# Adding an expert's rows to a copy of h in DRAM by an indirect DMA instead of scattering them on TensorE

## The reference, cut to what matters

```python
def moe_swiglu(x, w_router, w_in, w_out):      # x: 256 tokens x 1024
    logits = (xt @ w_router)
    top_v, top_i = lax.top_k(logits, 2)        # 2 of 8 experts for each token
    gates = one_hot(top_i) * softmax(top_v)    # summed over the two: 256 x 8
    for e in range(8):                         # w_in[e]: 1024 x 7168, w_out[e]: 3584 x 1024
        y = y + gates[:, e:e + 1] * swiglu(xt, w_in[e], w_out[e])
...
h = h + moe_swiglu(rms_norm(h, m_norm_g[j]), m_w_router[j], m_w_in[j], m_w_out[j])
```

## Time and profile before

| | |
|---|---|
| median of 3 runs | 1932.05 us (1930.89 to 1932.68) |
| the profiled execution | 1930.93 us, of which the trace's span is 1928.9 us |
| TensorE busy | 1882.8 us, 98% of the span |
| DVE busy | 1438.2 us, 75% |
| ACT busy | 1217.9 us, 63% |
| POOL busy | 32.4 us, 2% |
| chain that ended last | PE 93%, DVE 3%, ACT 3% |
| DMA | 508.12 MB, mean 263 GB/s over the span |

### The profile page before, as it was taken

One profiled execution on the slowest core, in us unless ns is written; L12 is line 12 of the kernel. 1 busy time (PEld: TensorE's weight loads), 2 busy tenths in 40 slices (PEclk: granted clock), 3 DMA queues, 4 the chain that ended last, 5 costly groups with the idle time before them and its releaser, 6 DMA issues.

```text
span 1928.9 us, 25964 instructions
## 1 busy us (share of the span) xinstructions
PE 1882.8 (98%) x8896; PEld 1569.7 (81%) x8896; DVE 1438.2 (75%) x1660; ACT 1217.9 (63%) x1360; POOL 32.4 (2%) x49
## 2 busy tenths in 40 slices
PE   8999999999998999999999999999999999999998
PEld 7998888888786888888888888888888878777887
DVE  5565476557666889888898888988989885577643
ACT  5544365447754777677777777777777765556542
POOL 2000000000000000000000000000000000000000
PEclk9999999999998999999999999999999999999999
DMA  8655555554247999999999999999999953345551
GB/s 266 181 189 202 191 185 186 177 176 155 104 143 274 363 383 353 376 365 363 385 349 376 363 364 384 351 376 366 365 380 350 373 204 121 110 135 160 175 176 43
DMA packets 234949, 508.12 MB, mean 263 GB/s; under 512 B 14332, under 2 KB 54352, under 8 KB 234880
## 3 DMA queue, kind: packets, MB, share of 16 engines
q1 hardware_dynamic: 232304, 499.70, 73.0%
q0 software_dynamic: 2272, 6.47, 1.1%
q10 hardware_dynamic: 304, 1.05, 0.2%
HBM read 505.07 MB, written 2.10 MB: 263 GB/s over the span
## 4 chain that ended last, share of the span: by engine, by line
PE 93%; DVE 3%; ACT 3%; issue 1%; DMA 0%; DVEq 0%; SPq 0%; ACTq 0%
PE G L1338 23%; PE G L1340 23%; PE G L1339 22%; PE SM L1338 5%; PE SM L1340 5%; PE SM L1339 5%; PE T L1298 3%; PE T L1724 1%; PE SM L1332 1%; ACT dense_high L453 1%; PE SM L1506 1%; DVE e_low L663 0%; PE G L1845 0%; DVE dense_low L464 0%; PE SM L1704 0%
## 5 line engine op out<-in xcount | busy, mean ns | idle before, releaser
L663 DVE TENSOR_TENSOR e_low<-e_arrived,e_high 128x2048 fp32r<-128x2048 f32 x338 | 756.1, 2286 | 81.1 <-ACT e_high L658 80.6
L658 ACT CAST e_high<-e_arrived 128x2048 fp32r<-128x2048 f32 x338 | 623.9, 1914 | 0.9 <-PE G L1340 0.8
L1338 PE MATMUL G<-e_high,work_r 128*128 128x512 f32 x896 | 355.8, 397 | 4.7 <-DVE routing L2473 4.7
L1340 PE MATMUL G<-e_high,work_r 128*128 128x512 f32 x896 | 350.1, 391 | 0.0
L1339 PE MATMUL G<-e_low,work_r 128*128 128x512 f32 x896 | 349.5, 390 | 0.0
L1338 PE MATMUL G<-dense_high,xT_hi_all 128*128 128x512 f32 (+1 forms) x760 | 295.9, 389 | 4.9 <-DVE dense_low L464 3.7
L1340 PE MATMUL G<-dense_high,xT_lo_all 128*128 128x512 f32 (+1 forms) x760 | 285.1, 375 | 0.0
L1339 PE MATMUL G<-dense_low,xT_hi_all 128*128 128x512 f32 (+1 forms) x760 | 284.1, 374 | 0.0
L464 DVE TENSOR_TENSOR dense_low<-dense_raw,dense_high 128x2048 fp32r<-128x2048 f32 (+1 forms) x74 | 150.5, 2059 | 99.7 <-ACT dense_high L446 97.7
L1338 PEld LDWEIGHTS G<-e_high,work_r 128*128 128x128 f32 x896 | 168.7, 188 | 40.0 <-issue 4.9
L1340 PEld LDWEIGHTS G<-e_high,work_r 128*128 128x128 f32 x896 | 168.6, 188 | 36.3
(11 more groups left out here) (336 smaller groups left out, 2076.3 us busy)
## 6 DMA issues: line engine op xcount, KB each, us to landing
e_arrived<-in_m_w_in_dram SPq DMA_DIRECT2D x448, 512.0 KB, 5.0
e_arrived<-in_m_w_out_dram SPq DMA_DIRECT2D x224, 512.0 KB, 5.0
dense_raw<-in_a_w_in_dram SPq DMA_DIRECT2D x32, 768.0 KB, 4.9
dense_raw<-in_f_w_in_dram SPq DMA_DIRECT2D x44, 512.0 KB, 4.6
dense_raw<-in_w_up_dram SPq DMA_DIRECT2D x16, 1024.0 KB, 5.2
dense_raw<-in_w_down_dram SPq DMA_DIRECT2D x16, 1024.0 KB, 4.8
dense_raw<-in_a_w_out_dram SPq DMA_DIRECT2D x12, 1024.0 KB, 4.9
dense_raw<-in_f_w_out_dram SPq DMA_DIRECT2D x11, 1024.0 KB, 4.9
```

Of the source, the lines that this page charges most:

```text
L658: nc.scalar.copy(e_hi_unit(n), e_raw(n, e_arrived)).then_inc(e_hi, 1)
L663: nc.vector.tensor_tensor(e_raw(n, e_low), e_raw(n, e_arrived), e_hi_unit(n).bitcast(F32), ALU.subtract).then_inc(e_lo, 1)
L1338: nc.tensor.matmul(bank, x_hi, w_hi, start=start, stop=False)
L1340: return nc.tensor.matmul(bank, x_lo, w_hi, start=False, stop=stop)
```

## The change

A second DRAM tensor `sums` (256 rows and 128 spare ones) takes a copy of `h` ahead of the loop. At the end of a pass ACT multiplies the expert's rows by a column of gates, one per slot (`row_gate`), into `y_rows`, and in the next pass POOL adds these rows to `sums` by an indirect DMA that accumulates (`compute_op=ALU.add`), with the row numbers in `row_to`; slots that hold no token go to a spare row of their own. Row numbers and gates come from four small fp32 matmuls behind unit 1 (`row_slots`) into bank T0 and three DVE operations of one column behind the making of units 6 and 7. Since `e_turn(it, 0)` writes T0 again, it now waits for these (`slots_ready`). `y_lo`, both scatters of a pass and DVE's four additions to `h` go out of the loop; only the last expert's rows are still split, scattered and added on chip, on top of the `h` that POOL brings back from `sums`. The turn of `pick` ("route") stays in the loop.

```diff
+        sums = nc.dram_tensor("sums", (S + P, D), F32, kind="Internal").ap()
...
+            for c in range(NT):
+                pool.dma_start(sums[c * P:(c + 1) * P, :], h[:, c, :]).then_inc(rows_saved, 16)
-            pool.wait_ge(rows_saved, 16 * NT)
+            pool.wait_ge(rows_saved, 32 * NT)
...
             with pool.Fori(0, rounds * E) as it:
+                pool.wait_ge(y_taken, it * 2 + 2)
+                pool.wait_ge(slots_ready, it + 1)
+                pool.sem_inc(sums_asked, 1)
+                pool.indirect_dma_start(sums, bass.IndirectOffsetOnAxis(row_to[:, :], 0), y_rows, None, compute_op=ALU.add
+                                        ).then_inc(sums_added, 16)
                 pool.wait_ge(index_ready, it + 1)
...
+            pool.wait_ge(sums_added, rounds * (16 * E))
+            for c in range(NT):
+                pool.dma_start(h[:, c, :], sums[c * P:(c + 1) * P, :]).then_inc(sums_landed, 16)
...
-                act.wait_ge(scatter_full, it * 4 + 4)
+                act.wait_ge(sums_added, it * 16 + 16)
                 for b in range(2):
                     act.wait_ge(y_full, it * 2 + b + 1)
-                    nc.scalar.copy(y_hi[:, b * BANK:(b + 1) * BANK], SM[b][:, :]).then_inc(y_hi_ready, 1)
+                    nc.scalar.mul(y_rows[:, b * BANK:(b + 1) * BANK], SM[b][:, :], row_gate[:, 0:1]).then_inc(y_taken, 1)
+            act.wait_ge(y_taken, rounds * (2 * E) + 2)
+            for b in range(2):
+                nc.scalar.copy(y_hi[:, b * BANK:(b + 1) * BANK], SM[b][:, :]).then_inc(y_hi_ready, 1)
...
+            def row_slots(it):
+                pe.wait_ge(gates_ready, 1)
+                pe.wait_ge(pick_ready, it + 1)
+                pe.wait_ge(e_turned_lo, it * DOWNS)
+                for c in range(NT):
+                    nc.tensor.matmul(T[0][:, 0:2], pick[:, c, :], token_one[:, c, :], start=(c == 0), stop=(c == NT - 1))
+                for c in range(NT):
+                    ins = nc.tensor.matmul(T[0][:, 2:3], pick[:, c, :], gate[:, c, bass.ds(it + 1, 1)], start=(c == 0), stop=(c == NT - 1))
+                ins.then_inc(slots_full, 1)
...
             def e_turn(it, what):
                 g = TURN_OF[what]
+                if what == 0:
+                    pe.wait_ge(slots_ready, it + 2)
...
                         if s == 0 and part == 1:
-                            pe.wait_ge(y_lo_ready, it * 2 + 2)
-                            scatter(0, scatter_full, SM)
-                        if s == 0 and part == 3:
-                            pe.wait_ge(scatter_added, it * 4 + 2)
-                            scatter(1, scatter_full, SM)
+                            row_slots(it)
...
-            V.memset(y_hi.bitcast(F32), 0.0)
-            V.memset(y_lo.bitcast(F32), 0.0).then_inc(y_lo_ready, 1)
-            V.memset(routeT.bitcast(F32), 0.0).then_inc(y_lo_ready, 1)
+            V.memset(y_rows, 0.0).then_inc(y_taken, 2)
+            dve.wait_ge(token_ready, 2)
+            V.tensor_scalar(minus_spare[:, :], spare_row[:, :], -1.0, None, ALU.mult)
+            V.tensor_copy(row_to[:, :], spare_row[:, :]).then_inc(slots_ready, 1)
...
-                    if kind == "up" and s == 0:
-                        c = part // 2
-                        for b in range(2):
-                            dve.wait_ge(scatter_full, it * 4 + 2 * c + b + 1)
-                            dst = h[:, c, b * BANK:(b + 1) * BANK]
-                            V.scalar_tensor_tensor(out=dst, in0=SM[b][:, :], scalar=gate[:, c, bass.ds(it, 1)], in1=dst,
-                                                   op0=ALU.mult, op1=ALU.add).then_inc(scatter_added, 1)
+                    if (kind, s, part) == ("up", 1, 0):
+                        dve.wait_ge(slots_full, it + 1)
+                        dve.wait_ge(sums_added, it * 16 + 16)
+                        V.tensor_copy(row_gate[:, :], T[0][:, 2:3])
+                        steps_loop(V.scalar_tensor_tensor(out=sum_row[:, :], in0=T[0][:, 1:2], scalar=minus_spare[:, 0:1], in1=spare_row[:, :],
+                                                          op0=ALU.mult, op1=ALU.add), it)
+                        V.tensor_tensor(row_to[:, :], T[0][:, 0:1], sum_row[:, :], ALU.add).then_inc(slots_ready, 1)
...
-                for b in range(2):
-                    dve.wait_ge(y_hi_ready, it * 2 + b + 1)
-                    at = slice(b * BANK, (b + 1) * BANK)
-                    V.tensor_tensor(y_lo[:, at], SM[b][:, :], y_hi[:, at].bitcast(F32), ALU.subtract).then_inc(y_lo_ready, 1)
+            for b in range(2):
+                dve.wait_ge(y_hi_ready, b + 1)
+                at = slice(b * BANK, (b + 1) * BANK)
+                V.tensor_tensor(y_lo[:, at], SM[b][:, :], y_hi[:, at].bitcast(F32), ALU.subtract).then_inc(y_lo_ready, 1)
+            dve.wait_ge(sums_landed, 16 * NT)
```

More of the change, by code:

```diff
@@ L255, in build @@
         pos_i = sb("pos_i", [P, NT], I32)
-        token = sb("token", [P, NT])
+        token_one = sb("token_one", [P, NT, 2])
+        token = token_one[:, :, 0]
         token_of = sb("token_of", [P, 1], U32)
+        spare_row, minus_spare, row_gate, sum_row = (routing[:, n:n + 1] for n in range(152, 156))
+        row_to = sb("row_to", [P, 1], U32)
+        sums = nc.dram_tensor("sums", (S + P, D), F32, kind="Internal").ap()
         saved_rows = nc.dram_tensor("saved_rows", (S, D), F32, kind="Internal").ap()
@@ L545, in build @@
         token_ready = sem("token_ready")
+        gates_ready = sem("gates_ready")
+        slots_full = sem("slots_full")
+        slots_ready = sem("slots_ready")
+        sums_asked = sem("sums_asked")
+        sums_added = sem("sums_added")
+        sums_landed = sem("sums_landed")
+        sums_wanted = sem("sums_wanted")
         rows_saved = sem("rows_saved")
@@ L556, in build @@
         y_hi = work_r[:, 0:D]
+        y_rows = work_all[:, 0:D]
+        y_taken = sem("y_taken")
+        row_step = sem("row_step")
         routeT = work_r[:, 1024:1280]
@@ L837, in _ @@
                           allow_slow_non_contiguous=True).then_inc(small_landed, 16)
-            nc.gpsimd.iota(token[:, :], pattern=[[P, NT]], base=0, channel_multiplier=1,
+            steps.then(nc.gpsimd.memset(token_one[:, :, :], 1.0))
+            nc.gpsimd.iota(token, pattern=[[P, NT]], base=0, channel_multiplier=1,
+                           allow_small_or_imprecise_dtypes=True).then_inc(token_ready, 1)
+            nc.gpsimd.iota(spare_row[:, :], pattern=[[0, 1]], base=S, channel_multiplier=1,
                            allow_small_or_imprecise_dtypes=True).then_inc(token_ready, 1)
@@ L854, in _ @@
                                         ).then_inc(rows_landed, 16)
+            pool.wait_ge(sums_added, rounds * (16 * E))
+            pool.sem_inc(sums_wanted, 1)
+            for c in range(NT):
+                pool.dma_start(h[:, c, :], sums[c * P:(c + 1) * P, :]).then_inc(sums_landed, 16)
         @block.scalar
@@ L1725, in e_turn @@
                 ins.then_inc(e_turned, 1)
-            pe.wait_ge(token_ready, 1)
+            pe.wait_ge(token_ready, 2)
             pe.wait_ge(pick_ready, 1)
@@ L1764, in _ @@
                         if s == 0 and part == 0:
-                            pe.wait_ge(scatter_added, it * 4 + 4)
+                            pe.wait_ge(y_taken, it * 2 + 2)
                         if s == DOWNS - 2 and part == 1:
@@ L1783, in _ @@
             for b in range(2):
-                pe.wait_ge(y_lo_ready, rounds * (2 * E) + 2)
+                pe.wait_ge(y_lo_ready, b + 1)
                 pe.wait_ge(gathered[b], rounds * (2 * E) + 2)
@@ L2469, in _ @@
                                                   op0=ALU.mult, op1=ALU.add))
-            steps.then(V.tensor_copy(gate[:, :, E + 1:2 * E + 1], gate[:, :, 1:E + 1]))
+            V.tensor_copy(gate[:, :, E + 1:2 * E + 1], gate[:, :, 1:E + 1]).then_inc(gates_ready, 1)
             dve.wait_ge(rounds_ready, 1)
@@ L2473, in _, with steps_loop @@
             V.memset(tmp8, 0.0).then_inc(up_read, 2)
+            def steps_loop(ins, it):
+                ins.then_inc(row_step, 1)
+                dve.wait_ge(row_step, it + 1)
             with dve.Fori(0, rounds * E) as it:
```

## The result

The changed kernel takes 1965.21 us (median of 4 runs, 1959.69 to 1966.79); beside it the kernel before took 1932.31 (4 runs). The ratio is 1.0167, with a 95% interval of 1.0149 to 1.0185: the change costs 33 us (1.7%). The forecast was 1966, with a range of 1953 to 1980.

What follows compares the result with a forecast made beforehand. TensorE, busy all 121.20 us of a pass, sets the pace, but ACT and DVE feed it at some units. 24.0 wait + 9.6 clock - 0.3 head + 0.5 tail = 33.8 on 1930.9: 1964.7, median 1966, range 1953 to 1980.

Steps and rivals of the forecast that it cites:

- The wait: Ahead of the hidden block's turn, TensorE waits for DVE's slots_ready: 3.0 us a pass, 24.0 in eight.
- The clock: Behind the new idle of 3.8 us TensorE drops to half clock: 1.6 us in 6 of 8 passes, 9.6.
- a choice between two rows: Trace rows on clock loss after TensorE idles: lost after 4.69 us, kept after 2.57 us.
- The removed matmuls: Scatters behind units 1 and 3: 64 matmuls, 14.5 us, their effect already inside the 24.0 us of waiting.
- the full count: Rival: TensorE is full, so removed and added matmuls count in full, -6.5 us, 1925.5; chance 0.04.
- The four small ones: New row-number and gate matmuls behind unit 1: 1.0 us, covered by the wait for unit 2's low part.
- The add: POOL's accumulating DMA into sums: 16.4 us, bounds 8.2 to 24.6, hidden under a cover of 19.6 us.
- the rival built on it: The add lands late at DVE's wait, 5.0 us more per pass and more clock loss, 2012 us; chance 0.10.
- The traffic: The add's bytes beside the weights: 0.5 MB moved up to three times per pass of 42 MB, costing nothing.
- The head: Ahead of the loop, DVE's memsets shrink: -0.3 us, bounds -0.9 to 0.
- The tail: Behind the loop, ACT multiplies twice before it copies: +0.5 us for the last scatter, bounds 0 and 1.3.
- the sum: Whole execution: wait, clock, head and tail add 33.8 us to the profiled 1930.9, giving 1964.7.

Runs made afterwards that it cites:

- experiment 1: Changed kernel with the four small matmuls writing bank SM1 instead of T0 and no wait ahead of the turn: 1928.03 us, ratio 0.9983 to the kernel before.
- experiment 2: Changed kernel with DVE's three one-column operations moved behind the low parts of units 4 and 5, bank T0 kept: 1929.25 us, ratio 0.9986.
- experiment 4: Changed kernel with fifteen matmuls, results never read, ahead of TensorE's wait for slots_ready: 1953.93 us, ratio 1.0119 to the kernel before.
- experiment 3: Kernel before without the eight passes' 64 scatter matmuls and DVE's additions to h: 1927.97 us, ratio 0.9982.
- experiment 5: Changed kernel without the loop's accumulating DMA, its semaphore raised by POOL itself: 1966.33 us, ratio 1.0171 to the kernel before.
- experiment 6: experiment 1 with the rows multiplied by their gates on DVE instead of ACT: 1929.03 us, ratio 0.9982 to the kernel before.
- experiment 7: experiment 6 plus a one-column Silu at the head of the loop's body: 1926.60 us, ratio 0.9967 to the kernel before.
- experiment 11: Changed kernel with the memsets of y_lo and routeT put back ahead of that of y_rows: 1966.48 us, one run.

## Why the prediction was right

**The wait.** Forecast: DVE, not TensorE, sets when the block is turned; 3.0 us a pass. Measured: 2.93, with TensorE idle 3.5 where 3.8 was said. The reason held in its parts. The high part of unit 6 is late because ACT waits for unit 3 and then loads Silu's table; removing DVE's additions does not bring it forward; the operations stand behind both low parts. Experiments 1 and 2 take the wait away in two ways and both return 35 to 37 us.

**The clock.** Forecast 6 of 8 passes at 1.6 us, 9.6 in all. Six of eight it was in the trace, five at 1.57 us and one at 2.6, 10.4 in all; experiment 4 puts it at 10.4 to 11.3. That it would be six was a choice between two rows, not a derivation, and the count was in part luck: the granted clock of the fastest run shows that it is not six in every execution. The waits of the two passes that kept the clock were as long (3.50 and 3.54 us) as those of the six that lost it (3.50 to 3.53), and what decides between them no run here shows. The rule of the Trainium skill (TensorE: Matmul & The Clock Gate, HAM oscillation), taken as a cold start after every such gap, would have given eight; this trace does not bear it out.

**The removed matmuls.** Forecast: in this kernel they bring nothing of their own. In experiment 3 they bring 0.5 us of 1.8 a pass, so even in a kernel without any new wait the full count would have been wrong by more than two thirds. The four small ones were put at 1.0 us: from the start of the first, at 866.87, to unit 2 at 867.92 are 1.05 with the wait of 0.19 in it.

**The add.** Forecast: hidden, with a duration of two fetches, 16.4 us, and a bound of 24.6. Hidden it was, but it takes 8.7 us, about one fetch. The estimate was twice too large and the rival built on it (0.10) had less ground than I gave it; experiment 5 puts its price at nothing. Experiments 6 and 7 show that the mechanism exists: when the landing goes to 16 us, DVE does wait for it. The traffic was put at up to three times 0.5 MB per add. The profile's counters have 7.34 MB written with the adds and 3.15 without them (experiment 5), 0.5 MB for each, and the same 506.12 MB read; a read of the target does not show in them.

**Head and tail.** This is where a term was mis-sized. The head was forecast at -0.3, with a bound of -0.9; the trace has -1.25. I had counted the two memsets as partly covered by other waits. In fact DVE's first addition to `h` comes 1.25 us sooner as well (579.88, before 581.13), and experiment 11 shows the memsets on DVE's path, so one memset of 0.91 and its issue, and the small one, count in full. The tail at +0.5 came out at +0.3. Left out of the sum altogether were the 2.6 us behind the loop and the 0.6 of clock at its beginning. Between the two profiled executions the sum was forecast at 33.8 us and is 35.9, of 36.1 in span. That 1966 fell within 1 us of the median is then partly luck: the profiled execution of the changed kernel lies 1.6 us above its median, where I had added 1.1 us because that of the kernel before lies below.

## What to carry to other kernels

Before counting what an edit takes from the busiest engine, ask which engine ends the wait at that place; here two others fed it just in time, and 64 matmuls were worth less than a third of their price. A scratch bank that is also the target of the next critical step turns a slow reader's place in its program into a wait of the busiest engine: put such a result into a bank that is needed late, or its reader early. And a new idle time on TensorE can have a second price in its clock (here 1.6 us behind an idle time of 3.5, in six of eight passes); where it can't be removed, matmuls that fill it can pay.

## What the runs showed of the hardware

An indirect DMA that accumulates 128 rows of 4 KB in DRAM lands 0.7 us later than a gather of as many rows: 8.7 us against 8.0 (medians), in passes that move 359 GB/s in all. Its issue takes POOL less time, 1.58 against 2.2 us.

The same issue took 9.38 us where it started 1 us inside a chain of four low parts on DVE (seven passes of experiment 6, seven of experiment 7). The Trainium skill (SBUF — State Buffer, the section on its two separate sides) has a rule for this: DVE and GpSimd share one pair of ports, under an exclusive lock that an instruction of DVE with two inputs in on-chip memory holds against a GpSimd operation that reads there. The fourteen passes agree with it. But the fetch, issued at 676.39 beside two low parts that began at 675.44, took 2.21 us, and the first pass's add took 1.88 beside four of them. So when DVE's chain shuts POOL out, and when not, stays open, and with it whether the rule is the cause.

Seen in every pass: ACT loads two tables of 1.28 us, one ahead of the first copy to a high part and one ahead of the first Silu. Later copies and Silus of the same pass follow each other without a load, so the copies also run with the table that the Silu needs. One column of Silu at the head of the body makes one load go away. It shortens a pass by 0.3 us on top of experiments 1 and 2, about 2 us in eight passes (the medians fall by 3.3 and 4.5, on different chips), and by nothing in the kernel before.
